# The last expert's rows kept apart: norm and store of all rows moved beside the last expert's matmuls

## The chip, the cores and the metric

The kernel runs on one core of one Trainium2 chip. The metric is device time in microseconds (us) of one whole execution; the kernel before took 3894.26 us (median of 3 runs, 3893.9 to 3895.97). All arithmetic here is in fp32.

## The reference

Two network blocks run one after the other on a sequence of 1024 tokens of 1024 features. The change touches only the end of the second block: a mixture of 16 experts in which each expert picks its own 128 tokens, and the final norm over all 1024 rows.

```python
def expert_choice_ffn(h, router_w, w_gate, w_up, w_down):
    cap = EC_CAPACITY * T // N_EXPERTS            # 2 * 1024 / 16 = 128
    aff = softmax(h @ router_w)
    gate, idx = lax.top_k(swapaxes(aff, 1, 2), cap)
    xe = h[idx]                                    # per expert: 128 rows
    hid = silu(xe @ w_gate) * (xe @ w_up)          # 1024 -> 512
    ye = (hid @ w_down) * gate                     # 512 -> 1024
    return zeros((T, D)).at[idx].add(ye)

# end of second_block
x = x + m_lat[5] * expert_choice_ffn(h_lat, ...)
return rms_norm(x, final_norm_g)                   # each row on its own
```

A token can be picked by several experts, so its row receives several additions. Within one expert's list every token stands once. The final norm needs the whole sum of a row.

## The kernel before, in words

The experts and the final norm are one function, `experts_and_norm`. Each of the five engines has an instruction list of its own, and they meet by semaphores; no scheduler moves anything, so the order of the code is the order on each engine.

**Experts.** For expert n, GpSimd (POOL) gathers 128 rows of `h` into `xe` with an indirect DMA. TensorE (PE) transposes them, and multiplies them with the gate weights (`ps_g`) and the up weights (`ps_u`), 8 matmuls of 128x512 each. ScalarE (ACT) takes the silu of `ps_g`, VectorE (DVE) multiplies it with `ps_u` into `hid`, PE transposes it into `ps_h`, ACT copies that to `hidT`, and PE multiplies with the down weights into the two banks `ps_d[0]` and `ps_d[1]`. DVE scales both banks into `ye`. POOL then adds `ye` onto the rows of `total` in DRAM with an accumulating indirect DMA (L5138; `total` is the tensor `x3`, which the profile prints as `x`). `added` counts these: the scatter of expert n waits until all n scatters before it have landed. PE goes on with the next expert meanwhile. Weights are double buffered; SyncE (SP) loads those of expert n + 2 when expert n is multiplied (L5051, L5052).

**Final norm.** SP waits until all 16 scatters have landed (`added` at 16 x 16), and then issues eight loads of 128 rows (512 KB each) into `tt` (L5109). For each of the eight tiles ACT squares with a sum (L5228) and takes the root (L5230); the first root needs another activation table than the silu. DVE takes the reciprocal (L5196) and multiplies the tile by it and by the gain (L5198). SP stores tile after tile to `out` as `normed` rises (L5112), waits for all stores, and the program ends.

Of the kernel before, what the change touches and what calls it, by code (L numbers as in the profile page):

```python
# [683 lines left out]
TILES = SEQ // P  # L684
# [4378 lines left out]
def experts_and_norm(nc, tag, h, idx, gates, weights, w_gate, w_up, w_down, total, ada, ada_bias, gate_at, gain, out):  # L5063
# [3 lines left out]
    with ExitStack() as ctx:  # L5067
# [14 lines left out]
        act_g, hid, hidT = sb("act_g", [P, FF]), sb("hid", [P, FF]), sb("hidT", [P, FB, P])  # L5082
        tt = sb("tt", [P, TILES, D])
        junk = sb("junk", [P, D], mybir.dt.bfloat16)
        ss, std, rstd, eps = (sb(n, [P, TILES]) for n in ("ss", "std", "rstd", "eps"))
        ps_t = [pbank("ps_t0"), pbank("ps_t1")]
        ps_g, ps_u, ps_h = pbank("ps_g"), pbank("ps_u"), pbank("ps_h")
# [5 lines left out]
        gathered = [sem("gathered0"), sem("gathered1")]  # L5093
        t_loaded = [sem(f"t_loaded{t}") for t in range(TILES)]
        stored = sem("stored")
        block = ctx.enter_context(nc.Block())

        @block.sync
        def _(sp):
            for n, src in enumerate((ada[0, gate_at:gate_at + D], ada_bias[gate_at:gate_at + D], gain)):  # L5100
                sp.dma_start(vecs[:, n, :], row_to_all(src, D)).then_inc(vecs_loaded, 16)
            with sp.Fori(0, EXPERTS // 2 - 1) as i:
                for b in range(2):

                    sp.wait_ge(d_made, 2 * i + b + 1)
                    load_expert(sp, weights, w_gate, w_up, w_down, 2 * i + (b + 2), b)
            sp.wait_ge(added, 16 * EXPERTS)
            for t in range(TILES):
                sp.dma_start(tt[:, t, :], total[t * P:(t + 1) * P, :]).then_inc(t_loaded[t], 16)  # L5109
            for t in range(TILES):  # L5110
                sp.wait_ge(normed, t + 1)
                sp.dma_start(out[t * P:(t + 1) * P, :], tt[:, t, :]).then_inc(stored, 16)  # L5112
            sp.wait_ge(stored, 16 * TILES)

        @block.gpsimd
        def _(pool):
            pool.memset(hold[:, :], 0.0)
            pool.memset(zero[:, :], 0.0)
            pool.memset(eps[:, :], EPS2)
            pool.drain()  # L5120

            def gather(b, e):


                pool.drain()
                pool.wait_ge(idx_set, e + 1)
                pool.tensor_tensor(hold[:, 0:1], zero[0:1, 0:1], zero[0:1, 0:1], ALU.add)
                pool.indirect_dma_start(out=xe[b][:, :], out_offset=None, in_=h,
                                        in_offset=bass.IndirectOffsetOnAxis(ap=idx_in[b][:, 0:1], axis=0)).then_inc(gathered[b], 16)

            def scatter(n, b):
                pool.drain()
                pool.wait_ge(y_done, n + 1)
                pool.tensor_tensor(hold[:, 0:1], zero[0:1, 0:1], zero[0:1, 0:1], ALU.add)

                pool.wait_ge(added, 16 * n)
                pool.tensor_tensor(hold[:, 1:2], zero[0:1, 0:1], zero[0:1, 0:1], ALU.add)
                pool.indirect_dma_start(out=total, out_offset=bass.IndirectOffsetOnAxis(ap=idx_out[b][:, 0:1], axis=0),  # L5138
                                        in_=ye[b][:, :], in_offset=None, compute_op=ALU.add).then_inc(added, 16)

            make_identity(pool, ident)
            pool.memset(ident[0:1, 0:1], 1.0).then_inc(consts, 1)
            gather(0, 0)
            gather(1, 1)
            with pool.Fori(0, EXPERTS // 2 - 1) as i:
                for b in range(2):
                    gather(b, 2 * i + (b + 2))
                    scatter(2 * i + b, b)
            scatter(EXPERTS - 2, 0)
            scatter(EXPERTS - 1, 1)  # L5150
            pool.wait_ge(added, 16 * EXPERTS)

        @block.vector
        def _(dve):
            def choose(b, e):

                dve.tensor_copy(idx_in[b][:, :], idx[:, bass.ds(e, 1)]).then_inc(idx_set, 1)

            choose(0, 0)
            choose(1, 1)  # L5160
            dve.wait_ge(vecs_loaded, 48)
            dve.tensor_tensor(vecs[:, 0, :], vecs[:, 0, :], vecs[:, 1, :], ALU.add)
            dve.drain()
# [26 lines left out]
                one(i, 0, True)  # L5190
                one(i, 1, True)
            one(EXPERTS // 2 - 1, 0, False)
            one(EXPERTS // 2 - 1, 1, False)
            for t in range(TILES):
                dve.wait_ge(std_done, t + 1)
                dve.reciprocal(rstd[:, t:t + 1], std[:, t:t + 1])  # L5196
                dve.drain()
                dve.scalar_tensor_tensor(out=tt[:, t, :], in0=tt[:, t, :], scalar=rstd[:, t:t + 1], in1=vecs[:, 2, :],  # L5198
                                         op0=ALU.mult, op1=ALU.mult).then_inc(normed, 1)

        @block.scalar
        def _(act):
            def move_x(n, b):
                for g in range(2):
                    act.wait_ge(turned, 2 * n + g + 1)
                    act.activation(xT[:, b, 4 * g:4 * g + 4, :], ps_t[g][:, :].rearrange("p (j c) -> p j c", j=4), ACT.Copy).then_inc(t_moved, 1)  # L5206

            def one(i, b, more):
                n = 2 * i + b
                act.wait_ge(g_made, n + 1)  # L5210
                act.wait_ge(hid_done, n)
                act.activation(act_g[:, :], ps_g[:, :], ACT.Silu).then_inc(g_act, 1)
                if more:
                    move_x(n + 1, 1 - b)
                act.wait_ge(h_turned, n + 1)
                act.wait_ge(d_made, n)
                act.activation(hidT[:, :, :], ps_h[:, :].rearrange("p (j c) -> p j c", j=FB), ACT.Copy).then_inc(h_moved, 1)  # L5217

            move_x(0, 0)
            with act.Fori(0, EXPERTS // 2 - 1) as i:  # L5220
                one(i, 0, True)
                one(i, 1, True)
            one(EXPERTS // 2 - 1, 0, True)
            one(EXPERTS // 2 - 1, 1, False)
            act.wait_ge(consts, 1)
            for t in range(TILES):
                act.wait_ge(t_loaded[t], 16)
                act.activation(junk[:, :], tt[:, t, :], ACT.Square, accum_out=ss[:, t:t + 1])  # L5228
                act.drain()
                act.activation(std[:, t:t + 1], ss[:, t:t + 1], ACT.Sqrt, scale=1.0 / D, bias=eps[:, 0:1]).then_inc(std_done, 1)  # L5230

        @block.tensor
        def _(pe):
# [9 lines left out]
                        last = pe.transpose(ps_t[g][:, j * P:(j + 1) * P], xe[b][:, k * P:(k + 1) * P], ident[:, :])  # L5243
                    last.then_inc(turned, 1)

            def one(i, b, more):
                n = 2 * i + b
                pe.wait_ge(gu_loaded[b], 32 * i + 32)
                pe.wait_ge(t_moved, 2 * n + 2)
# [18 lines left out]
                for g in range(2):  # L5268
                    for j in range(FB):
                        last = pe.matmul(ps_d[g][:, :], hidT[:, j, :], wd[:, b, j, g * BANK:(g + 1) * BANK], start=(j == 0), stop=(j == FB - 1))  # L5270
                last.then_inc(d_made, 1)

            turn(0, 0, 0)
            with pe.Fori(0, EXPERTS // 2 - 1) as i:
                one(i, 0, True)
                one(i, 1, True)
            one(EXPERTS // 2 - 1, 0, True)
            one(EXPERTS // 2 - 1, 1, False)


Z_WIDTH = 384
# [153 lines left out]
```

## Time and profile before

| What | us |
|---|---|
| Median of 3 runs | 3894.26 (3893.9 to 3895.97) |
| The profiled execution, its own time | 3900.91 |
| Its span (first to last instruction) | 3899.2 |
| PE busy in the span | 3479.7 (89%) |
| DVE, ACT, POOL busy | 1947.2 (50%), 1086.2 (28%), 1238.5 (32%) |

The profile is of one execution, 6.65 us above the median of the runs shown. Times in it count from the first instruction. A busy engine is one whose instructions run; waiting is not counted. The engine PE is busy nearly everywhere except in the last stretch, where it has nothing to do: its last matmul begins in a group at 3857.32 us and ends at 3864.5 us, 34.7 us before the span's end.

### The profile page before, as it was taken

The page shows a single profiled execution, that of the slowest core. Times are in us where ns is not written, and L with a number is a line of the kernel's source. Part 1 is how long each engine was busy: PE and PEld are TensorE (multiplying, and loading weights), DVE is VectorE, ACT ScalarE, POOL GpSimd, SP SyncE. Part 2 cuts the span into 40 slices and gives each one's busy share as a digit, 9 for nine tenths or more (in the row PEclk, how much of TensorE's full clock was granted, in tenths as well). Part 3 has the DMA queues.
Part 4 walks back from the last instruction along what each step waited for, and adds up shares of the span by engine and source line. Part 5 has one row for each costly group of instructions (what it writes and reads, how often), then busy time and mean ns, then how long its engine had stood idle before and what let it go on. Part 6 is the DMA issues. An engine that isn't in the chain of part 4 may idle for free. (4 is left out here: it accounts for less than half of the span.)

```text
span 3899.2 us, 47844 instructions
## 1 busy us (share of the span) xinstructions
PE 3479.7 (89%) x16721; PEld 2282.8 (59%) x16721; DVE 1947.2 (50%) x4099; ACT 1086.2 (28%) x2196; POOL 1238.5 (32%) x979
## 2 busy tenths in 40 slices
PE   8999998999798999999989798999977877939996
PEld 3745776777344676576657346575577874524442
DVE  2036663543783376667686453426588586141111
ACT  1024333441341233333342351322113112201111
POOL 2110101433343455556555452002302553201110
PEclk9999998999899999999999898999988878969998
DMA  4264543231532121221211643123325703438996
GB/s 134 79 181 132 168 122 100 87 108 64 220 146 65 59 59 42 63 58 53 74 41 37 250 161 92 44 79 106 126 76 180 252 33 143 163 127 288 315 317 227
DMA packets 417492, 494.07 MB, mean 127 GB/s; under 512 B 71042, under 2 KB 321178, under 8 KB 417267
## 3 DMA queue, kind: packets, MB, share of 16 engines
q1 hardware_dynamic: 390695, 463.64, 35.9%
q0 software_dynamic: 4608, 16.78, 1.7%
q10 hardware_dynamic: 21964, 10.75, 1.0%
q8 instruction: 129, 2.11, 0.2%
q14 instruction: 96, 0.79, 0.1%
HBM read 362.32 MB, written 128.77 MB: 126 GB/s over the span
## 5 line engine op out<-in xcount | busy, mean ns | idle before, releaser
L1091 POOL TENSOR_TENSOR hgrn_queries<-hgrn_qd,hgrn_pair_decay 128x640 f32<-128x640 f32 x192 | 262.7, 1387 | 293.5 <-PE hgrn_ps_a L1206 252.2
L1141 PE MATMUL hgrn_ps_w<-xT,hgrn_ring 128*128 128x512 f32 x432 | 196.4, 601 | 1.8 <-PEq L34 1.8
L415 PE MATMUL gla_bg_ps<-gla_bg_w,xT 128*128 128x256 f32 x768 | 186.2, 387 | 0.0
L554 POOL TENSOR_TENSOR l_wsum<-l_ring 128x512 f32<-128x512 f32 x14 | 20.0, 1430 | 507.4 <-PE att_bg_ps L586 185.6
L1757 PE MATMUL end_ps_z<-end_w,end_yT 128*128 128x512 f32 x384 | 168.8, 599 | 1.4 <-ACT end_yT L1700 1.4
L2927 PE MATMUL end_ps_z<-end_w,end_yT 128*128 128x512 f32 x384 | 166.8, 594 | 1.5 <-ACT end_yT L2847 1.5
L415 PEld LDWEIGHTS gla_bg_ps<-gla_bg_w,xT 128*128 128x128 f32 x768 | 145.7, 194 | 26.0 <-issue 6.8
L1311 DVE TENSOR_TENSOR hgrn_k_end<-hgrn_kd,hgrn_end_decay 128x128 f32<-128x128 f32 x168 | 136.2, 850 | 9.2 <-issue 2.6
L1141 PEld LDWEIGHTS hgrn_ps_w<-xT,hgrn_ring 128*128 128x128 f32 x432 | 81.7, 194 | 94.5 <-issue 94.2
L2205 ACT ACTIVATE att_s_sb<-att_s_sb,att_shift 128x256 f32<-128x256 f32 (+1 forms) x192 | 88.9, 464 | 166.2 <-DVE att_shift L2162 166.1
L1141 PE MATMUL hgrn_ps_w<-hgrn_xs,hgrn_wsum 128*128 128x512 f32 x288 | 130.0, 599 | 4.8 <-ACT hgrn_sig L1425 4.8
L1146 PE MATMUL hgrn_ps_w<-hgrn_ring,xT 128*128 128x256 f32 x576 | 129.7, 381 | 0.0
L1757 PEld LDWEIGHTS end_ps_z<-end_w,end_yT 128*128 128x128 f32 x384 | 73.0, 192 | 92.2 <-issue 89.1
L3328 PE MATMUL in_ps<-hT_cols,in_w 128*128 128x512 f32 x288 | 126.2, 592 | 0.0
L2172 DVE SCALAR_TENSOR_TENSOR att_acc<-att_w_ada,sT,att_acc 128x256 f32<-128x256 f32 x224 | 118.7, 543 | 14.3 <-issue 0.9
L2927 PEld LDWEIGHTS end_ps_z<-end_w,end_yT 128*128 128x128 f32 x384 | 72.3, 190 | 90.9 <-issue 87.8
L5270 PE MATMUL exp_ps_d<-expw_wd,exp_hidT 128*128 128x512 f32 x256 | 114.1, 599 | 11.0 <-ACT exp_hidT L5217 11.0
L1146 PEld LDWEIGHTS hgrn_ps_w<-hgrn_ring,xT 128*128 128x128 f32 x576 | 108.7, 192 | 14.5 <-issue 0.5
L2380 POOL TENSOR_TENSOR gla_queries<-gla_qd,gla_pair_decay 128x640 f32<-128x640 f32 x64 | 90.9, 1440 | 80.9 <-PE gla_ps_o L2446 57.2
L5252 PE MATMUL exp_ps_g<-expw_wg,exp_xT 128*128 128x512 f32 x256 | 115.4, 605 | 0.7 <-ACT exp_xT L5206 0.7
L2097 PE MATMUL att_ps_s<-att_k,att_q 64*128 64x256 f32 (+1 forms) x384 | 90.4, 553 | 25.5 <-DVE att_shift L2162 25.4
L5256 PE MATMUL exp_ps_u<-expw_wu,exp_xT 128*128 128x512 f32 x256 | 112.5, 592 | 0.0
(692 smaller groups left out, 7825.7 us busy)
## 6 DMA issues: line engine op xcount, KB each, us to landing
expw_wg<-in_exp_w_gate_dram SPq DMA_DIRECT2D x16, 2048.0 KB, 9.7
expw_wu<-in_exp_w_up_dram SPq DMA_DIRECT2D x16, 2048.0 KB, 16.3
expw_wd<-in_exp_w_down_dram SPq DMA_DIRECT2D x16, 2048.0 KB, 21.8
att_w_ada<-in_ada_w_dram SPq DMA_DIRECT2D x24, 1024.0 KB, 6.4
hgrn_ring<-in_w_in_c_dram SPq DMA_DIRECT2D x18, 1024.0 KB, 5.4
l_ring<-in_w_in_ab_dram SPq DMA_DIRECT2D x14, 1024.0 KB, 5.6
end_gt<-gate_l SPq DMA_DIRECT2D x16, 768.0 KB, 8.1
hgrn_ring<-in_w_in_c_dram SPq DMA_DIRECT2D x24, 512.0 KB, 5.2
```

What stands on the lines that cost most here:

```text
L415: last = pe.matmul(bank[0:job.rows, q * job.width:(q + 1) * job.width], job.acts[:, k, t * P:t * P + job.rows], w[:, k, 0:job.width], star ...
L1091: pool.tensor_tensor(queries[:, d, s, :].rearrange("p (b a c) -> p b a c", b=POINTS, a=PC), q, f, ALU.mult).then_inc(queries_done, 1)
L1141: last = pe.matmul(bank[:, :], a[:, k, :], x(k), start=(fresh and k == 0), stop=(k == HK - 1), skip_group_check=True)
L1146: last = pe.matmul(bank[:, q * 2 * P:(q + 1) * 2 * P], x(k)[:, t * P:(t + 1) * P], a[:, k, :], start=(fresh and q == 0 and k == 0), stop=( ...
L1311: dve.tensor_tensor(k_end[:, d, p % 2, :].rearrange("p (a c) -> p a c", c=CH), kd[:, b, d, t * P:(t + 1) * P].rearrange("p (a c) -> p a c" ...
L1757: made = pe.matmul(ps_z[h][:, :], yT[:, k, :], w[:, k, h * BANK:(h + 1) * BANK], start=(k == 0), stop=(k == NB - 1))
L2172: last = dve.scalar_tensor_tensor(out=mine, in0=w, scalar=s, in1=mine, op0=ALU.mult, op1=ALU.add)
L2927: made = pe.matmul(ps_z[h][:, :], yT[:, k, :], w[:, k, halves[h]], start=(k == 0), stop=(k == NB - 1))
L3328: last = pe.matmul(ps[(3 * n + part) % 2][:, 0:span], w[u % 3][:, k, b * P:(b + 1) * P], acts, start=(k == 0), stop=(k == KB - 1))
L5252: last = pe.matmul(ps_g[:, :], xT[:, b, k, :], wg[:, b, k, :], start=(k == 0), stop=(k == KB - 1))
L5256: last = pe.matmul(ps_u[:, :], xT[:, b, k, :], wu[:, b, k, :], start=(k == 0), stop=(k == KB - 1))
L5270: last = pe.matmul(ps_d[g][:, :], hidT[:, j, :], wd[:, b, j, g * BANK:(g + 1) * BANK], start=(j == 0), stop=(j == FB - 1))
```

## The change

Only the last expert (number 15, called FINAL) and the norm are written anew; experts 0 to 14 stay as they were.

- SP waits for 15 scatters instead of 16, and then loads the eight tiles of `tt`, which lack expert 15's contribution.
- ACT takes the silu of expert 15, then square and root of tile 0, then the copy to `hidT` of expert 15, and then the other seven tiles.
- DVE normalises tiles 0 to 3 behind `hid` of expert 15, then handles the first half of expert 15's result, tiles 4 and 5, the second half, tiles 6 and 7.
- POOL no longer adds expert 15 into `total`. When 15 scatters have landed it gathers expert 15's 128 rows of `total` into a new tile `rows`. DVE adds expert 15's scaled result to them (`last_half`), ACT and DVE norm them apart, and POOL scatters them to `out`, when all eight stores of SP have landed. It then waits for that scatter.
- PE signals each of the two banks of expert 15 (`last_made`) instead of both together (`d_made`).

So 128 of the 1024 rows are stored twice: first without expert 15 by the tile stores, and then complete by the scatter.

```diff
@@ sync
-            sp.wait_ge(added, 16 * EXPERTS)
+            sp.wait_ge(added, 16 * FINAL)
             for t in range(TILES):
                 sp.dma_start(tt[:, t, :], total[t * P:(t + 1) * P, :]).then_inc(t_loaded[t], 16)
@@ gpsimd
             scatter(EXPERTS - 2, 0)
-            scatter(EXPERTS - 1, 1)
-            pool.wait_ge(added, 16 * EXPERTS)
+            pool.drain()
+            pool.wait_ge(last_set, 1)
+            pool.tensor_tensor(hold[:, 0:1], zero[0:1, 0:1], zero[0:1, 0:1], ALU.add)
+            pool.wait_ge(added, 16 * FINAL)
+            pool.tensor_tensor(hold[:, 1:2], zero[0:1, 0:1], zero[0:1, 0:1], ALU.add)
+            pool.indirect_dma_start(out=rows[:, :], out_offset=None, in_=total,
+                                    in_offset=bass.IndirectOffsetOnAxis(ap=idx_last[:, 0:1], axis=0)).then_inc(rows_gathered, 16)
+            pool.drain()
+            pool.wait_ge(last_normed, 1)
+            pool.tensor_tensor(hold[:, 0:1], zero[0:1, 0:1], zero[0:1, 0:1], ALU.add)
+            pool.wait_ge(stored, 16 * TILES)
+            pool.tensor_tensor(hold[:, 1:2], zero[0:1, 0:1], zero[0:1, 0:1], ALU.add)
+            pool.indirect_dma_start(out=out, out_offset=bass.IndirectOffsetOnAxis(ap=idx_last[:, 0:1], axis=0),
+                                    in_=rows[:, :], in_offset=None).then_inc(last_stored, 16)
+            pool.wait_ge(last_stored, 16)
@@ vector
-            one(EXPERTS // 2 - 1, 1, False)
-            for t in range(TILES):
+            def normalise(t):
                 dve.wait_ge(std_done, t + 1)
                 dve.reciprocal(rstd[:, t:t + 1], std[:, t:t + 1])
                 dve.drain()
                 dve.scalar_tensor_tensor(out=tt[:, t, :], in0=tt[:, t, :], scalar=rstd[:, t:t + 1], in1=vecs[:, 2, :],
                                          op0=ALU.mult, op1=ALU.mult).then_inc(normed, 1)
+            def last_half(g):
+                c = slice(g * BANK, (g + 1) * BANK)
+                dve.wait_ge(last_made, g + 1)
+                dve.scalar_tensor_tensor(out=ye[1][:, c], in0=ps_d[g][:, :], scalar=gate_now[:, 1:2], in1=vecs[:, 0, c], op0=ALU.mult, op1=ALU.mult)
+                if g == 0:
+                    dve.wait_ge(rows_gathered, 16)
+                dve.drain()
+                dve.tensor_tensor(rows[:, c], rows[:, c], ye[1][:, c], ALU.add).then_inc(last_added, 1)
+
+            dve.tensor_copy(gate_now[:, 1:2], gates[:, FINAL:EXPERTS])
+            ...
+            dve.tensor_tensor(hid[:, :], act_g[:, :], ps_u[:, :], ALU.mult).then_inc(hid_done, 1)
+            dve.wait_ge(added, 16 * (FINAL - 1))
+            for t in range(TILES):
+                if t == 4:
+                    last_half(0)
+                if t == 6:
+                    last_half(1)
+                normalise(t)
+            dve.wait_ge(last_squared, 2)
+            dve.tensor_tensor(last_ss[:, 0:1], last_ss[:, 0:1], last_ss[:, 1:2], ALU.add).then_inc(last_summed, 1)
+            dve.wait_ge(last_root, 1)
+            dve.reciprocal(last_rstd[:, 0:1], last_std[:, 0:1])
+            dve.drain()
+            dve.scalar_tensor_tensor(out=rows[:, :], in0=rows[:, :], scalar=last_rstd[:, 0:1], in1=vecs[:, 2, :],
+                                     op0=ALU.mult, op1=ALU.mult).then_inc(last_normed, 1)
@@ scalar
-            one(EXPERTS // 2 - 1, 1, False)
-            act.wait_ge(consts, 1)
-            for t in range(TILES):
+            def root(t):
                 ...
+            act.activation(act_g[:, :], ps_g[:, :], ACT.Silu).then_inc(g_act, 1)
+            root(0)
+            act.wait_ge(h_turned, EXPERTS)
+            act.wait_ge(d_made, FINAL)
+            act.activation(hidT[:, :, :], ps_h[:, :].rearrange("p (j c) -> p j c", j=FB), ACT.Copy).then_inc(h_moved, 1)
+            for t in range(1, TILES):
+                root(t)
+            for g in range(2):
+                act.wait_ge(last_added, g + 1)
+                act.activation(junk[:, 0:BANK], rows[:, g * BANK:(g + 1) * BANK], ACT.Square, accum_out=last_ss[:, g:g + 1]).then_inc(last_squared, 1)
+                act.drain()
+            act.wait_ge(last_summed, 1)
+            act.activation(last_std[:, 0:1], last_ss[:, 0:1], ACT.Sqrt, scale=1.0 / D, bias=eps[:, 0:1]).then_inc(last_root, 1)
@@ tensor, in one(i, b, more, final=False)
-                last.then_inc(d_made, 1)
+                    if final:
+                        last.then_inc(last_made, 1)
+                if not final:
+                    last.then_inc(d_made, 1)
```

Where instructions stand on an engine is shown at three places, first before and then now. On ScalarE, from the silu of expert 15 on (`act_g` is the silu's result, `hidT` the transposed hidden tile, `ss` the sum of squares, `std` the root):

```order
L5212 ACTIVATE exp_act_g<-exp_ps_g 128x512
L5217 ACTIVATE exp_hidT<-exp_ps_h 128x512
L5228 ACTIVATE exp_junk,exp_ss<-exp_tt 128x1024
L5230 ACT_TABLE_LOAD
L5230 ACTIVATE exp_std<-exp_ss,exp_eps 128x1
```

```order
L5282 ACTIVATE exp_act_g<-exp_ps_g 128x512
L5275 ACTIVATE exp_junk,exp_ss<-exp_tt 128x1024
L5277 ACT_TABLE_LOAD
L5277 ACTIVATE exp_std<-exp_ss,exp_eps 128x1
L5286 ACTIVATE exp_hidT<-exp_ps_h 128x512
```

The square, the table load and the root of tile 0 now stand between the silu and the copy that PE's last eight matmuls wait for, and no second table load stands behind them.

On VectorE, from `hid` of expert 15 on (before, the rows shown run from `hid` to the first tile of the norm; now, from the fourth tile over the first half of expert 15 to the fifth tile):

```order
L5176 TENSOR_TENSOR exp_hid<-exp_act_g,exp_ps_u 128x512
L5180 COPY exp_idx_out<-idx 128x1
L5183 SCALAR_TENSOR_TENSOR exp_ye<-exp_ps_d,exp_gate_now,exp_vecs 128x512 x2
L5196 RECIPROCAL exp_rstd<-exp_std 128x1
L5198 SCALAR_TENSOR_TENSOR exp_tt<-exp_tt,exp_rstd,exp_vecs 128x1024
```

```order
L5217 SCALAR_TENSOR_TENSOR exp_tt<-exp_tt,exp_rstd,exp_vecs 128x1024
L5223 SCALAR_TENSOR_TENSOR exp_ye<-exp_ps_d,exp_gate_now,exp_vecs 128x512
L5227 TENSOR_TENSOR exp_rows<-exp_rows,exp_ye 128x512
L5215 RECIPROCAL exp_rstd<-exp_std 128x1
L5217 SCALAR_TENSOR_TENSOR exp_tt<-exp_tt,exp_rstd,exp_vecs 128x1024
```

The two scalings of `ps_d` are now two separate steps, each with an add, that stand ahead of tiles 4 and 6 of the norm.

On GpSimd, the end of its list, behind the scatter of expert 14:

```order
L5134 TENSOR_TENSOR exp_hold<-exp_zero 1x1
L5137 TENSOR_TENSOR exp_hold<-exp_zero 1x1
L5138 DMA x<-exp_ye,exp_idx_out 1024x1024
```

```order
L5157 TENSOR_TENSOR exp_hold<-exp_zero 1x1
L5159 TENSOR_TENSOR exp_hold<-exp_zero 1x1
L5160 DMA exp_rows<-x,exp_idx_last 128x1024
L5164 TENSOR_TENSOR exp_hold<-exp_zero 1x1
L5166 TENSOR_TENSOR exp_hold<-exp_zero 1x1
L5167 DMA out_dram<-exp_rows,exp_idx_last 1024x1024
```

One accumulating scatter has become a gather and, at the very end, a plain scatter to the output.

## Rows read from the trace of the kernel before

**Rows 1.** The chain that ended last, at its end: start us, us, what.
```profile
3848.31 0.60 ACT exp_act_g L5212
3857.32 7.15 PE exp_ps_d L5270 x16
3864.64 1.33 DVE exp_ye L5183 x2
3865.97 0.07 issue
3866.04 0.18 POOL exp_hold L5134
3866.53 6.06 DMA x<-exp_ye,exp_idx_out
3872.60 3.18 DMA exp_tt<-x
3877.07 1.28 ACT L5230
3889.04 1.28 DVE exp_tt L5198
```

**Rows 2.** DMA, 3873 to 3897 us: share of 16 engines in 40 slices, GB/s, queues, issues.
```profile
DMA  0999999999999997999999999999999999999411
GB/s 20 266 355 410 382 335 341 355 389 389 403 410 410 423 410 253 259 212 287 335 389 416 423 403 403 423 430 416 416 430 403 423 430 417 430 410 423 164 48 48
DMA packets 2303, 8.39 MB, mean 350 GB/s; under 512 B 255, under 2 KB 255, under 8 KB 2302
...
out_dram<-exp_tt SPq DMA_DIRECT2D x8, 512.0 KB, 7.3
```

**Rows 3.** The line of the stores, and DMA 3890.3 to 3891: last store's us to landing.
```profile
L5112 SPq DMA_DIRECT2D out_dram<-exp_tt x8: 332/333/338, 3880.2 to 3890.4; - x8
...
out_dram<-exp_tt SPq DMA_DIRECT2D x1, 512.0 KB, 7.2
```

**Rows 4.** Timeline of VectorE, hid of expert 15, and the norm's beat.
```profile
3855.24 0.69 DVE L5176 TENSOR_TENSOR exp_hid<-exp_act_g,exp_ps_u 128x512 f32<-128x512 f32 x1 [12.26 <-issue]
3864.56 1.40 DVE L5183 SCALAR_TENSOR_TENSOR exp_ye<-exp_ps_d,exp_gate_now,exp_vecs 128x512 f32<-128x512 f32 x2
...
3880.14 0.15 DVE L5196 RECIPROCAL exp_rstd<-exp_std 128x1 f32<-128x1 f32 x1
3880.36 1.28 DVE L5198 SCALAR_TENSOR_TENSOR exp_tt<-exp_tt,exp_rstd,exp_vecs 128x1024 f32<-128x1024 f32 x1
3881.57 0.15 DVE L5196 RECIPROCAL exp_rstd<-exp_std 128x1 f32<-128x1 f32 x1
```

**Rows 5.** Timeline of GpSimd: the scatter of expert 14, then that of 15.
```profile
3843.49 1.57 POOL L5138 DMA_INDIRECT x<-exp_ye,exp_idx_out  x1 [0.16 <-issue]
...
3866.19 0.18 POOL L5137 TENSOR_TENSOR exp_hold<-exp_zero 1x1 f32<-1x1 f32 x1
3866.53 1.56 POOL L5138 DMA_INDIRECT x<-exp_ye,exp_idx_out  x1 [0.16 <-issue]
```

**Rows 6.** DMA, 3840 to 3860 us, same columns as rows 2.
```profile
DMA  0000000000095899940000000000000000100000
...
x<-exp_ye,exp_idx_out POOLq DMA_INDIRECT x1, 6.3
```

**Rows 7.** The line of the tile loads, L5109: min/median/max us to landing.
```profile
L5109 SPq DMA_DIRECT2D exp_tt<-x x8: 344/462/1084, 3872.6 to 3877.1; - x8
...
DMA to landing us min/median/max: 3.2/7.3/10.1
```

**Rows 8.** Timeline of ScalarE: the copy of expert 15, then the norm's first two tiles.
```profile
3856.67 0.60 ACT L5217 ACTIVATE exp_hidT<-exp_ps_h 128x512 f32<-128x512 f32 x1 [7.76 <-PE exp_ps_h L5263]
3875.86 1.06 ACT L5228 ACTIVATE exp_junk<-exp_tt 128x1024 bf16<-128x1024 f32 x1 [18.59 <-DMA exp_tt<-x]
3876.82 0.19 ACT L5228 ACTIVATION_READ_ACCUMULATOR exp_junk<-exp_tt 128x1 f32 x1
3877.07 1.28 ACT L5230 ACT_TABLE_LOAD   x1
3878.36 0.29 ACT L5230 ACTIVATE exp_std<-exp_ss,exp_eps 128x1 f32<-128x1 f32 x1
3878.57 1.04 ACT L5228 ACTIVATE exp_junk<-exp_tt 128x1024 bf16<-128x1024 f32 x1
```

**Rows 9.** Indirect gathers, L5128, 3480 to 3500 us: us to landing, min/median/max.
```profile
L5128 POOL DMA_INDIRECT exp_xe<-h,exp_idx_in x3: 956/962/1223, 3482.9 to 3495.9; - x3
...
DMA to landing us min/median/max: 4.3/4.3/7.0
```

**Rows 10.** All 16 gathers (L5128) and all 16 scatters (L5138).
```profile
DMA to landing us min/median/max: 4.3/7.3/8.7
...
DMA to landing us min/median/max: 6.1/10.1/10.3
```

**Rows 11.** Stores of 512 KB of another stage, L4821.
```profile
L4821 SPq DMA_DIRECT2D h<-mix_out x8: 325/326/339, 3314.7 to 3429.0; - x8
...
DMA to landing us min/median/max: 2.6/2.6/7.0
```

**Rows 12.** Windows: stretch, busy us by engine, then PEclk, DMA share, GB/s.
```profile
3818.50:3838.50 20.00, 19.31 (x54) 9.06 (x53) 2.21 (x5) 2.25 (x4) 1.92 (x3) 1.00 0.94 324
3509.70:3864.50 354.80, 342.94 (x918) 158.67 (x916) 34.61 (x90) 42.07 (x67) 43.96 (x71) 1.00 0.84 290
3434.00:3509.60 75.60, 21.71 (x56) 11.05 (x57) 39.93 (x101) 3.38 (x5) 4.44 (x12) 0.57 0.13 44
```

More of the change, by code:

```diff
@@ L5084, in experts_and_norm @@
         junk = sb("junk", [P, D], mybir.dt.bfloat16)
+        rows, idx_last = sb("rows", [P, D]), sb("idx_last", [P, 1], I32)
+        last_ss, last_std, last_rstd = (sb(n, [P, 2]) for n in ("last_ss", "last_std", "last_rstd"))
         ss, std, rstd, eps = (sb(n, [P, TILES]) for n in ("ss", "std", "rstd", "eps"))
@@ L5095, in experts_and_norm @@
         stored = sem("stored")
+        last_set, rows_gathered, last_made, last_added, last_squared, last_summed, last_root, last_normed, last_stored = (sem(n) for n in (
+            "last_set", "rows_gathered", "last_made", "last_added", "last_squared", "last_summed", "last_root", "last_normed", "last_stored"))
+        FINAL = EXPERTS - 1
         block = ctx.enter_context(nc.Block())
@@ L5160, in _ @@
             choose(1, 1)
+            dve.tensor_copy(idx_last[:, :], idx[:, FINAL:EXPERTS]).then_inc(last_set, 1)
             dve.wait_ge(vecs_loaded, 48)
@@ L5199, in _ @@
                                          op0=ALU.mult, op1=ALU.mult).then_inc(normed, 1)
+            def last_half(g):
[7 more added lines that the diff above has]
+            dve.tensor_copy(gate_now[:, 1:2], gates[:, FINAL:EXPERTS])
+            dve.wait_ge(g_act, EXPERTS)
+            dve.wait_ge(u_made, EXPERTS)
+            dve.wait_ge(h_turned, FINAL)
+            dve.tensor_tensor(hid[:, :], act_g[:, :], ps_u[:, :], ALU.mult).then_inc(hid_done, 1)
[13 more added lines that the diff above has]
+                                     op0=ALU.mult, op1=ALU.mult).then_inc(last_normed, 1)
         @block.scalar
@@ L5230, in _ @@
                 act.activation(std[:, t:t + 1], ss[:, t:t + 1], ACT.Sqrt, scale=1.0 / D, bias=eps[:, 0:1]).then_inc(std_done, 1)
+            act.wait_ge(consts, 1)
+            act.wait_ge(g_made, EXPERTS)
+            act.wait_ge(hid_done, FINAL)
+            act.activation(act_g[:, :], ps_g[:, :], ACT.Silu).then_inc(g_act, 1)
[11 more added lines that the diff above has]
+            act.activation(last_std[:, 0:1], last_ss[:, 0:1], ACT.Sqrt, scale=1.0 / D, bias=eps[:, 0:1]).then_inc(last_root, 1)
         @block.tensor
@@ L5244, in turn, with one @@
                     last.then_inc(turned, 1)
-            def one(i, b, more):
+            def one(i, b, more, final=False):
                 n = 2 * i + b
@@ L5277, in _ @@
             one(EXPERTS // 2 - 1, 0, True)
-            one(EXPERTS // 2 - 1, 1, False)
+            one(EXPERTS // 2 - 1, 1, False, True)
 Z_WIDTH = 384
```

## The prediction

> **What bounds the kernel now.** I read the page's busy shares first (TensorE 89%, so most of the program is TensorE's), then the chain of waits at the place of the change. That chain shows the end of the kernel as a serial tail in which TensorE does nothing: from the last matmul at 3864.5 us to the span's end at 3899.2 us lie 34.7 us [rows 1]. Its pieces are: DVE's scaling 1.5, POOL and the accumulating scatter 6.6 (3865.97 to 3872.60), the first tile's load 3.2, squares and first root with its table load 2.9, eight tiles of DVE at one per 1.43 us until 3890.33, and the last store. I then read the DMA view of 3873 to 3897 us: 8.39 MB move with the 16 DMA engines full in nearly every slice [rows 2]. So tail stores queue behind each other and behind loads; the last, issued at 3890.4, lands 7.2 us later, at 3897.6 [rows 3], and the program ends 1.6 us after it. Last, the DMA view of 3840 to 3860 us: the queues are empty beside the scatter of expert 14, while TensorE multiplies expert 15 [rows 6]. That is where the change puts the loads.
>
> **Experts 0 to 14.** Nothing changes there but one 128x1 copy on DVE at the start (0.15 us, beside waiting). The loop ends as before, and I keep its times.
>
> **Start of the loads.** The scatter of expert 14 starts at 3843.49 [rows 5] and takes 6.3 us [rows 6]: it lands at 3849.8. SP's queue holds nothing else then, so the eight loads start at 3849.8 instead of 3872.60. That is 22.8 us earlier, which is the most that the change could give if all else followed at once.
>
> **ACT, tile 0 and `hidT`.** The first load took 3.2 us [rows 7], so tile 0 is there at 3853.0; the silu ended at 3848.9 [rows 1]. Square, sum, table load and root took from 3875.86 to 3878.65, 2.8 us [rows 8]: until 3855.8. `hidT` waits for its transposes and started at 3856.67 [rows 8]. So root(0) lies in ACT's idle time with 0.85 us to spare, and TensorE isn't held. The cover is thin: every microsecond by which tile 0 lands later than 3.2 + 0.85 delays `hidT`, TensorE's last group of matmuls and all other roots by as much. Nothing is queued behind the wait on ACT but these.
> What the trace shows of the table load is 1.28 us and 0.06 us of issue ahead of it [rows 1, 8].
> The Trainium skill (ScalarE: Activation LUTs, What ACT_TABLE_LOAD costs) adds a drain of about 1.38 us to each switch. By the page, estimated, root(0) would end at 3857.2, `hidT` would be 0.6 us late and the gain 0.6 us smaller; the trace has no such gap at this very switch, so my sum leaves it out.
>
> **ACT, tiles 1 to 7.** They follow `hidT` (3857.27) at 1.40 us each (the second square starts at 3878.57 [rows 8], and DVE, fed by the roots, keeps 1.43 [rows 4]), with root(1) done 1.5 us after its start: 3858.8, then to 3867.2 for tile 7. The loads keep ahead: at the 350 GB/s of [rows 2] 4.2 MB take 12 us, and 13.5 with the 0.5 MB gather; tile 7 is needed at 3865.7.
>
> **DVE.** `hid` ends at 3855.93 [rows 4]. Tile 0 goes 3855.9 to 3857.5, then DVE waits for root(1) at 3858.8. From there a tile costs 1.43 us (3880.14 to 3881.57) [rows 4]. Each half of expert 15 costs a scaling, 0.74 (1.40 for two that overlap), a drain of about 0.07 and an add of 0.69 (taken from `hid`, the same shape): 1.5 us. The halves start at 3863.1 and 3867.5. `ps_d[0]` is ready at 3857.32 + 3.6 = 3860.9 and `ps_d[1]` at 3864.5, so neither waits. The gather of `rows` starts with about 0.5 us for POOL at 3850.3; gathers took 4.3 us with free queues [rows 9] and at most 8.7 beside weight loads [rows 10]: it lands at 3859 at the latest, 4 us ahead of need. Tile 7 is normed at 3858.8 + 7 x 1.43 + 2 x 1.5 + 0.1 = 3871.9. Without the two halves it would be 3868.9.
>
> **The last store.** Issued at 3872.0 instead of 3890.4. Stores now come from DVE at 1.43 us and more apart, while 512 KB take 1.3 us at the 410 GB/s of the full slices [rows 2]. The loads and the gather are through by 3863.5, and the four stores then waiting by 3869, so tile 7 meets a nearly empty queue. Bounds: 2.6 us for a store with free queues [rows 11], 7.2 for one in a full queue [rows 3]. I take 3.0, near the first: landed at 3875.0.
>
> **The last 128 rows.** ACT's second half-square runs beside tiles 6 and 7. After tile 7, DVE's sum 0.2, ACT's root 0.35, reciprocal, drain and scaling 1.55: `rows` is ready at 3874.0, 1.0 us before the stores have landed. So the stores decide, not the norm. POOL then needs about 0.4 us (3866.19 to 3866.53 before) [rows 5], and scatters from 3875.4. The trace has no plain scatter. Below: a gather of the same 128 rows, 4.3 [rows 9]. Above: the accumulating scatter, 6.1 at the least, which reads before it writes, and 10.1 beside loads [rows 10]. There are no loads then. Its issue is 0.6 us longer than a gather's (1.57 against 0.96) [rows 5, 9], which makes 4.9 my value, nearest the gather. Landed at 3880.3, and 1.6 us to the end: 3881.9.
> [...]
>
> **Sum.** 3899.2 - 3881.9 = 17.3 us less span. The profiled execution took 3900.91, so it would take 3883.6; the runs shown have a median 6.65 us below that: 3894.26 - 17.3 = 3877.0 us. In terms: loads earlier 22.8, minus two halves 2.9, minus ACT's pause before tile 1 (root(1) ends 5.8 us after load 0 has landed, before 4.3) 1.5, minus POOL and scatter 5.3, plus a store that doesn't queue 4.2.
>
> **Rivals.**
> (a) *DMA and tile 0 go as in the full stretch.* Tile 0 lands later, ACT is held in root(0), `hidT` and the roots slip; and the last store queues. For it: thin cover of 0.85 us, the gather of `rows` and the tile loads start in the same microsecond, so 0.5 MB more shares the DMA engines. Against: the first load before had seven others behind it too. Price: tile 0 at 5.2 instead of 3.2 costs 1.2; a last store at 7.2 costs 4.2 more; a scatter of 6.1 costs 1.2. Together 6.6: 3883.6 us.
> (b) *The plain scatter is as dear as the loaded one*, 10.1: 5.2 more, 3882.2 us. With (a)'s store it is 3886.4, the edge of what is told from no change. It has no loads beside it, so this is unlikely.
> (c) *Slower: TensorE's clock.* The experts run at the full level, 2.4 GHz (granted 1.00 over 354.8 us), and the 75.6 us before them, in which TensorE was busy 21.7 us, at 0.57 [rows 12]. TensorE fills these 354.8 us; if the new build were granted 1.2 GHz in part of them, each microsecond so spent costs half of one. It decides from 35 us at the lower level on; a stretch of 75 us would cost 38 and give 3915 us. For it: the clock is granted by the chip, not set. Against: nothing before 3848 changes, and TensorE's own gaps stay.
> (d) *TensorE slows beside the tile loads.* It ran 19.31 of 20 us beside weight loads that took 0.94 of the DMA engines [rows 12], so I give it nothing.
> (e) *The old tail stays*, because something still waits for expert 15 before the stores. The order shows all eight tile norms independent of it except through DVE's two halves, so it costs 3 us, already counted.
>
> **How the numbers follow.** This kernel's measurement tells 0.2%, some 7.8 us, from no change. My forecast 0.76, with its own range of 3875.0 to 3880.5 (store 2.6 to 5, scatter 4.3 to 6.1, tile 0 up to 1 us late). (a) 0.13, (b) 0.05, (c) 0.03, anything else that leaves it within 0.2%: 0.03. The range reaches up to (a): 3874.8 to 3883.8. Faster by over 0.2%: forecast, (a) and most of (b), 0.93. Same 0.04, slower 0.03.
>
> **What would show it.** Tile loads issued at about 3849.8, square of tile 0 at 3853, `hidT` still at 3856.7 (at 3857.3 or later, the cover was too thin). TensorE's last matmul still ends at 3864.5. DVE in one beat from 3858.8 to 3872 with no wait but the one before tile 1. The last tile store lands 3 us after issue. POOL's wait is ended by the stores and not by DVE. The plain scatter takes 4.3 to 6.1 us, and the span ends 1.6 us later, near 3882. The prediction is wrong if DVE waits for `rows` or for `ps_d`, if ACT holds TensorE, or if the stretch before 3843 us moves.

## The result, and the profile after

The changed kernel took 3873.22 us (median of 4 runs, 3870.82 to 3873.76) against 3895.11 us before (4 runs, 3893.9 to 3897.46): ratio 0.9947, 95% interval 0.9935 to 0.9958. Faster, as forecast, but by 21.9 us where 17.3 were forecast. The forecast was 3877.0 us; the result lies 1.8 us below its own range (3875.0 to 3880.5) and 1.6 us below the range with rival (a) in it (3874.8 to 3883.8).

The end of the chain of waits of the changed kernel, in the columns of [rows 1] (`...` stands for pieces left out):

```profile
3838.95 0.61 ACT exp_act_g L5282
...
3849.53 1.28 DVE exp_tt L5217
...
3861.38 1.30 DVE exp_tt L5217
3862.68 0.02 issue
3862.70 3.65 DMA out_dram<-exp_tt
3866.34 0.07 issue
3866.41 0.18 POOL exp_hold L5166
3866.59 0.16 issue
3866.75 1.00 POOL out_dram L5167
```

The accumulating scatter (6.06) and the first tile's load (3.18) are gone from the chain. VectorE's tiles now stand beside the last expert, and the tail store (7.2 in [rows 3]) has become 3.65. The timeline of GpSimd has the three issues that matter, and that of SyncE the loads and stores:

```profile
3834.08 1.59 POOL L5143 DMA_INDIRECT x<-exp_ye,exp_idx_out  x1 [0.16 <-issue]
...
3841.44 1.00 POOL L5160 DMA_INDIRECT exp_rows<-x,exp_idx_last  x1 [0.39 <-issue]
...
3866.41 0.18 POOL L5166 TENSOR_TENSOR exp_hold<-exp_zero 1x1 f32<-1x1 f32 x1 [1.52 <-DMA out_dram<-exp_tt]
3866.75 1.00 POOL L5167 DMA_INDIRECT out_dram<-exp_rows,exp_idx_last  x1 [0.16 <-issue]
```

```profile
3840.57 4.00 SPq L5114 DMA_DIRECT2D exp_tt<-x  x8
3848.44 14.59 SPq L5117 DMA_DIRECT2D out_dram<-exp_tt  x8
```

Here is the surprise. The scatter of expert 14 belongs to code that the change doesn't touch, and it is issued at 3834.08, where [rows 5] has 3843.49. So the two profiled spans differ by 27.2 us: 9.4 ahead of the change and 17.8 in it. (The medians differ by less, 21.9 us, because the profiled execution of the kernel before was a long one.) Measured from that scatter's issue to the end of the span, the tail was 55.7 us and is 37.9.

| From the issue of the scatter of expert 14 | before | forecast | after |
|---|---|---|---|
| tile loads issued | 29.1 | 6.3 | 6.5 |
| `hidT` of expert 15 | 13.2 | 13.2 | 13.2 |
| second tile begun on DVE | 36.7 | 15.3 | 15.2 |
| tile 7 normed, store issued | 46.9 | 28.5 | 28.6 |
| last tile store landed | 54.1 | 31.5 | 32.3 |
| plain scatter issued | - | 31.9 | 32.7 |
| plain scatter landed | - | 36.8 | 36.1 |
| end of the span | 55.7 | 38.4 | 37.9 |

ScalarE around the copy, to set beside [rows 8]:

```profile
3843.99 1.06 ACT L5275 ACTIVATE exp_junk<-exp_tt 128x1024 bf16<-128x1024 f32 x1 [4.44 <-DMA exp_tt<-x]
3844.95 0.19 ACT L5275 ACTIVATION_READ_ACCUMULATOR exp_junk<-exp_tt 128x1 f32 x1
3845.19 1.28 ACT L5277 ACT_TABLE_LOAD   x1
3846.49 0.29 ACT L5277 ACTIVATE exp_std<-exp_ss,exp_eps 128x1 f32<-128x1 f32 x1
3847.26 0.60 ACT L5286 ACTIVATE exp_hidT<-exp_ps_h 128x512 f32<-128x512 f32 x1 [0.48 <-PE exp_ps_h L5327]
```

ScalarE waited 0.48 us for `ps_h` after the root of tile 0. The cover (the idle time of ScalarE in which the root of tile 0 hides) held, with half of the 0.85 us that I had given it. And the DMA view from 3841 to 3865 us, to set beside [rows 2]:

```profile
DMA  1599999999999999999999999999999999899897
...
DMA packets 2442, 8.91 MB, mean 371 GB/s; under 512 B 270, under 2 KB 270, under 8 KB 2440
```

The DMA engines are as full as they were, now from the first load to the last store: the last two slices still have 9 and 7 tenths, where I had forecast a nearly empty queue for the last store.

### The profile page after: what moved, and what is told of

Its sections match the earlier page's. It is cut to its first block and busy times, and to the rows that moved or that the text cites. A ratio compares the mean times of both kernels' runs of the same rounds, so it can differ in the third digit from the quotient of the medians.

```text
span 3872.0 us, 47862 instructions
## 1 busy us (share of the span) xinstructions
PE 3474.3 (90%) x16721; PEld 2277.8 (59%) x16721; DVE 1949.0 (50%) x4104; ACT 1088.4 (28%) x2201; POOL 1242.9 (32%) x982
## 6 DMA issues: line engine op xcount, KB each, us to landing
expw_wd<-in_exp_w_down_dram SPq DMA_DIRECT2D x16, 2048.0 KB, 21.9
```

## The experiments

Theory A: the change is worth its tail, about 18 us, and what lies ahead of it takes a different time in every execution. Theory B: the changed program is also faster ahead of expert 15, by the same amount each time. "Tail" is always the time from the issue of the scatter of expert 14 to the end of the span, read from the run's one profile. Ratios are to the kernel before, run in the same session.

**e1: the kernel before, unchanged.**

> The kernel before, unchanged. Theory A (drift): the stages ahead of expert 15 take a different time from execution to execution, because the granted clock falls and rises at other places in the stretch from 2680 to 3060 us; the change is worth only its tail, 17.8 us. Then the scatter of expert 14 is issued anywhere between 3834 and 3844 us in this profile, and the ratio to the kernel before is 1.000 within 0.0015. Theory B (build): the changed program is faster ahead of expert 15 by a fixed amount. Then the scatter of expert 14 is issued at 3843.5 +- 1.5 us here, as in the first trace of before. Both expect 55.7 +- 0.5 us from that issue to the end of the span.

Ratio 0.9998 (0.9987 to 1.0008), 12 runs from 3886.24 to 3899.76. Scatter of expert 14 at 3839.50, tail 55.4. The same program was 4.0 us earlier at that scatter than in the first trace: theory A's kind of difference, larger than B allows.

**e2: the changed kernel, unchanged.**

> The changed kernel, unchanged. Theory A (drift): ratio to before between 0.9944 and 0.9960 (17.8 us is 0.9954), issue of the scatter of expert 14 anywhere between 3834 and 3844 us. Theory B (build): ratio 0.9944 or below again, and that issue at 3834 +- 1.5 us. Both expect 37.9 +- 0.5 us from that issue to the end of the span.

Ratio 0.9953 (0.9940 to 0.9965), 5 runs from 3871.31 to 3875.32. Scatter at 3832.53, tail 37.1. The two signs point to different theories: the ratio is A's, though its interval reaches B's 0.9944, and the scatter is 1.5 us earlier than A allowed and just inside B's 3834 +- 1.5. The tail came out 0.3 us shorter than the 37.4 to 38.4 expected of both, because the last store landed 2.9 us after its issue and not 3.65.

**e3: only the declarations of the change.**

```diff
+        rows, idx_last = sb("rows", [P, D]), sb("idx_last", [P, 1], I32)
+        last_ss, last_std, last_rstd = (sb(n, [P, 2]) for n in ("last_ss", "last_std", "last_rstd"))
+        last_set, rows_gathered, last_made, last_added, last_squared, last_summed, last_root, last_normed, last_stored = (sem(n) for n in (
...
+            dve.tensor_copy(idx_last[:, :], idx[:, FINAL:EXPERTS]).then_inc(last_set, 1)
```

> The kernel before with only the new tiles, the nine new semaphores and the one 128x1 copy of the last expert's indices. Theory A (drift): ratio 1.000 within 0.0015. Theory B (build), in the form that the new declarations or the moved addresses do it: ratio 0.9985 to 0.9990 (4 to 6 us faster), and the scatter of expert 14 issued near 3834 us. The tail of 55.7 us stays under both.

Ratio 1.0003 (0.9992 to 1.0015), scatter at 3837.46, tail 55.5. New tiles, semaphores and moved addresses give nothing beyond 0.1%, so theory B in this form is out.

**e4: the loads held back.**

```diff
             sp.wait_ge(added, 16 * FINAL)
+            sp.wait_ge(last_made, 2)
@@ scalar
-            root(0)
...
-            for t in range(1, TILES):
+            for t in range(TILES):
                 root(t)
```

> The changed kernel with the tile loads held back until both banks of expert 15 are multiplied, and root(0) behind the copy to hidT (it would wait for itself otherwise). If the gain comes from moving the tile loads beside expert 15's matmuls: loads issue 14.5 us later, tile 0 is normed about 13 us later, the stores again share the DMA engines with the loads and the last one lands 3 to 4 us later after its issue: 37.9 + 16.5 = 54 to 55 us from the issue of the scatter of expert 14 to the end, ratio to before 0.9990 to 1.0005. Rival: the gain comes from not waiting for the last scatter (6.6 us) and not from the overlap: then some 44 us and a ratio near 0.997.

Ratio 0.9988 (0.9978 to 0.9998), tail 50.6. The first two rows are SyncE's, the third is VectorE's first tile:

```profile
3854.64 3.73 SPq L5115 DMA_DIRECT2D exp_tt<-x  x8
3862.35 13.61 SPq L5118 DMA_DIRECT2D out_dram<-exp_tt  x8
```

```profile
3861.03 1.28 DVE L5218 SCALAR_TENSOR_TENSOR exp_tt<-exp_tt,exp_rstd,exp_vecs 128x1024 f32<-128x1024 f32 x1
```

Loads at 21.1 us after the scatter instead of 6.5, and tile 7 13.4 us later, as expected. But the last store landed 3.2 us after its issue, not 7, and the tail is 3.4 us shorter than the 54 expected at the least. From the first load's issue to the last store's issue 21.0 us pass, where 17.8 passed before, and the two halves are 3.0 of that; so the stores come slowly enough for the queue to empty (no run of e4 without the halves shows it apart). Of the 18 us, then, 13.0 come from the overlap (50.6 against a mean of 37.6 in four profiles of the changed kernel; e4 moves root(0) too, which alone cost 2.05 in e6), and some 5 are left when nothing overlaps. Those 5 are a sum: the loads 8.1 us earlier, since no scatter of expert 15 stands ahead of them, and a last store that lands 4.0 us faster; against that 3.2 more up to the last store's issue, and 3.7 more behind its landing, where the plain scatter now stands. The overlap is most of the gain; of the rival's 11.5 us, less than half came.

**e5: the changed kernel again.**

> The changed kernel once more. Theory A (drift: the stages ahead take what the clock gives them in each execution, the same for both programs): median ratio to before 0.9954 +- 0.001, and with more runs the spread grows to that of before, 10 us and more between lowest and highest. Theory B (this program is steadier and some 3 us faster ahead of expert 15): ratio 0.9946 or below, all runs again within 5 us. Both expect 37.1 to 37.9 us from the issue of the scatter of expert 14 to the end of the span.

Ratio 0.9949 (0.9932 to 0.9965), 6 runs from 3869.04 to 3880.80, scatter at 3832.72, tail 37.9. The spread grew to 11.8 us, which takes away the narrow times of theory B. The ratio lies inside A's 0.9944 to 0.9964 and just above B's 0.9946; its interval holds both.

**e6: `root(0)` behind the copy to `hidT`** (the ScalarE part of e4's diff alone).

> The changed kernel with root(0) behind the copy to hidT instead of ahead of it. If the beat of VectorE, which starts at the second tile's root, sets the tail: square, table load and root of tile 0 (2.9 us) now come after hidT, every tile is normed 2.8 us later, and the tail is 40.3 us instead of 37.5. Rival: the DMA engines, full from the first load to the last store, set the tail, and VectorE's delay is hidden in them: tail 38.0 us or less.

Ratio 0.9966 (0.9954 to 0.9978), tail 39.65. VectorE's tiles 1 to 7 all came 2.8 us later, as the first theory said. The last store then took 2.6 us to land instead of the 2.9 to 3.65 of the changed kernel, so 2.05 us of it were lost in the end (39.65 against the mean of 37.6), between the 40.3 of the one theory and the 38.0 of the other. Both have their part: VectorE's beat (its steady 1.43 us for each tile), cushioned by full DMA engines. This is also the price of the cover: were root(0) not hidden ahead of `hidT`, 2 us of the gain would be gone.

**e7: both halves of expert 15 behind tile 7. e8: the first ahead of tile 7, the second behind.**

```diff
             for t in range(TILES):
-                if t == 4:
-                    last_half(0)
-                if t == 6:
-                    last_half(1)
                 normalise(t)
+            last_half(0)
+            last_half(1)
```

```diff
             for t in range(TILES):
-                if t == 4:
+                if t == 7:
                     last_half(0)
-                if t == 6:
-                    last_half(1)
                 normalise(t)
+            last_half(1)
```

> The changed kernel with both halves of expert 15 behind tile 7 on VectorE. If VectorE's beat alone set the last store, it would be issued 2.9 us earlier and land 2.9 us earlier; then the last rows decide, ready about 1 us ahead of the old landing: tail 0.7 us shorter. Rival: the DMA engines are full, the last store is issued 2.9 us earlier but lands at most 1 us earlier (landing 5.5 us or more after issue instead of 3.65): tail shorter by 0.7 us as well, but the wait ahead of the scatter is then ended by the store or within 0.3 us of it.

> The changed kernel with the first half of expert 15 ahead of tile 7 and the second behind it. The last store is issued 1.4 us earlier than in the changed kernel; the rows are ready at the same time as in e7. Both theories of e7 expect a tail 0.7 us shorter than the changed kernel's; if the DMA engines set the store's landing, it comes within 0.5 us of that in e7 although it is issued 1.5 us later.

e7: ratio 0.9950 (0.9934 to 0.9966), tail 38.0. e8: 0.9959 (0.9944 to 0.9974), tail 37.9. No gain in either, where both theories had expected a tail 0.7 us shorter. The last store's landing, from the views of the DMA issues around it, first e7, then e8:

```profile
out_dram<-exp_tt SPq DMA_DIRECT2D x1, 512.0 KB, 6.3
```

```profile
out_dram<-exp_tt SPq DMA_DIRECT2D x1, 512.0 KB, 5.1
```

In the changed kernel, e8 and e7 the last store is issued 28.6, 27.2 and 26.1 us after the scatter of expert 14, and it lands at 32.3, 32.3 and 32.4 us. When VectorE finishes doesn't matter in this span of 2.5 us. (With the issue always at 28.6, the landing itself lies between 31.5 and 32.3 in the four profiles of the changed kernel.) The rival of e7 held in what it said of the store, and so did e8's landing within 0.5 us of e7's; the shorter tail that went with them did not come.

**e9: as e7, the stores of tiles 0, 2 and 4 left out.** Part of the output is then not written. The two waits for all stores count five instead of eight (not shown).

```diff
             for t in range(TILES):
-                sp.wait_ge(normed, t + 1)
-                sp.dma_start(out[t * P:(t + 1) * P, :], tt[:, t, :]).then_inc(stored, 16)
+                if t not in (0, 2, 4):
+                    sp.wait_ge(normed, t + 1)
+                    sp.dma_start(out[t * P:(t + 1) * P, :], tt[:, t, :]).then_inc(stored, 16)
```

> As e7 (both halves of expert 15 behind tile 7), and the stores of tiles 0, 2 and 4 are left out, so part of the output isn't written; 1.5 MB less go through the DMA engines. If full DMA engines held the last store in e7 (6.3 us from issue to landing), it now lands 2.6 to 3.7 us after issue; the last rows then decide, and the tail from the issue of the scatter of expert 14 is 37.3 to 37.7 us. Rival: a store's landing near the end is slow for another reason than traffic; then it stays at 6 us.

Ratio 0.9951 (0.9932 to 0.9969), only 2 runs. The last store landed 2.6 us after its issue, 28.4 us after the scatter: 4.0 us earlier than in e7. The 1.5 MB left out are 3.9 us at some 400 GB/s, but that the two agree is partly luck: 2.6 us is what a store takes with free DMA engines [rows 11], so here its issue sets the landing and no longer the bytes. The wait ahead of the final scatter was then ended by the rows:

```profile
3868.88 0.18 POOL L5165 TENSOR_TENSOR exp_hold<-exp_zero 1x1 f32<-1x1 f32 x1 [23.47 <-DVE exp_rows L5245]
3869.02 0.18 POOL L5167 TENSOR_TENSOR exp_hold<-exp_zero 1x1 f32<-1x1 f32 x1
```

Tail 36.9, 0.4 under the 37.3 to 37.7 expected. So traffic holds the last store of the changed kernel: its landing is bound by the bytes from the first load on. The tail as a whole is held only a little by them. With the store 4.0 us earlier it became 1.1 us shorter than in e7, because the rows of expert 15 come right behind, and e6 shows that a later VectorE costs at once.

**e10: experts 14 and 15 both apart.** The way tried next is to start the bytes earlier. Rows of expert 14 (`pre_rows`) are treated like those of expert 15 and scattered ahead of them, and VectorE and ScalarE handle all eight tiles ahead of expert 15's silu and `hid`.

```diff
-            sp.wait_ge(added, 16 * FINAL)
+            sp.wait_ge(added, 16 * (FINAL - 1))
@@ gpsimd
+            for t in range(TILES):
+                pool.wait_ge(t_loaded[t], 16)
+            pool.tensor_tensor(hold[:, 0:1], zero[0:1, 0:1], zero[0:1, 0:1], ALU.add)
             scatter(EXPERTS - 2, 0)
...
+            pool.indirect_dma_start(out=pre_rows[:, :], out_offset=None, in_=total,
+                                    in_offset=bass.IndirectOffsetOnAxis(ap=idx_out[0][:, 0:1], axis=0)).then_inc(pre_gathered, 16)
...
+            pool.indirect_dma_start(out=out, out_offset=bass.IndirectOffsetOnAxis(ap=idx_out[0][:, 0:1], axis=0),
+                                    in_=pre_rows[:, :], in_offset=None).then_inc(pre_stored, 16)
```

> Experts 14 and 15 both kept apart: the tile loads start when 14 scatters have landed and end before the scatter of expert 14, all eight tiles are normed before hid of expert 15, and the rows of expert 14 and of expert 15 are gathered, normed and scattered one after the other. If the tail of the changed kernel is held by the 8.9 MB that move from the first load on, starting them one expert earlier takes it away: the last matmul's end to the end of the span falls from 16.9 us to some 12.6 us, and the ratio to before is near 0.9943. Rival: the longer chain on GpSimd (two gathers, two scatters, about 4 us each) takes the place of the stores, and that time stays at 16 us or more.

Ratio 0.9964 (0.9952 to 0.9976), 6 runs with a mean of 3878.8: 4.0 us above the changed kernel in the same session (e11), with an uncertainty of about 1.4. GpSimd's timeline says part of why:

```profile
3844.84 2.55 POOL L5146 DMA_INDIRECT x<-exp_ye,exp_idx_out  x1 [0.16 <-issue]
3854.30 0.18 POOL L5164 TENSOR_TENSOR exp_hold<-exp_zero 1x1 f32<-1x1 f32 x1 [6.92 <-issue]
...
3855.02 1.00 POOL L5167 DMA_INDIRECT exp_rows<-x,exp_idx_last  x1 [0.39 <-issue]
3856.33 0.98 POOL L5169 DMA_INDIRECT exp_pre_rows<-x,exp_idx_out  x1 [0.30 <-issue]
...
3866.27 1.00 POOL L5176 DMA_INDIRECT out_dram<-exp_pre_rows,exp_idx_out  x1 [0.16 <-issue]
3870.05 0.18 POOL L5180 TENSOR_TENSOR exp_hold<-exp_zero 1x1 f32<-1x1 f32 x1 [2.78 <-DVE exp_rows L5265]
...
3870.54 1.00 POOL L5183 DMA_INDIRECT out_dram<-exp_rows,exp_idx_last  x1 [0.16 <-issue]
```

The scatter of expert 14 had to wait for the tile loads, which shared the engines with expert 15's weights, until 3843. Its landing (3854.1) and the two gathers then stood in a row. But the final scatter did not wait for the one ahead of it, which had landed at 3869.6: its wait was ended at 3870.05 by VectorE. The chain shows what stood between the second gather and the end:

```profile
3856.33 5.01 DMA exp_pre_rows<-x,exp_idx_out
...
3861.36 1.06 ACT exp_junk L5308
...
3862.56 1.28 ACT L5310
...
3864.42 1.28 DVE exp_pre_rows L5257
...
3866.44 0.70 DVE exp_rows L5243
...
3868.68 1.29 DVE exp_rows L5265
```

The norm of expert 14's rows, with a table load (the 1.28 us of L5310) that the changed kernel doesn't have there, stood on ScalarE and VectorE ahead of expert 15's second half. `hid` came late too, behind the tiles, and TensorE waited 1.9 us for it where it had waited 0.8. From the last matmul's end (3857.9) to the end 17.9 us passed, against 16.9 in the first profile of the changed kernel (16.1 to 16.9 in its four). The rival of e10 held in its time, 16 us or more, and half in its reason: two gathers in a row, but not two scatters. None of the versions tried beats the changed kernel.

**e11: the changed kernel a fourth time.**

> The changed kernel a fourth time. Theory A (drift): the mean over its runs stays 17.8 +- 2.5 us below that of the kernel before on the same chip, and the issue of the scatter of expert 14 lies anywhere between 3828 and 3846 us. Theory B (3 us more ahead of expert 15): 20.5 us or more below again.

Ratio 0.9953 (0.9939 to 0.9966), mean 3874.8 over 5 runs against 3892.1 of before: 17.3 us. Scatter of expert 14 at 3837.66, tail 37.5. Both signs are theory A's.

**All runs together.** Taking each program's tail from its mean time leaves what lies ahead: before 3893.34 - 55.55 = 3837.8 (53 runs, spread 21.8 us; 3838.0 if the 28 runs of the first comparison, e1 and e3 are added); changed 3873.58 - 37.60 = 3836.0 (20 runs, spread 11.8 us); e4, e6, e7 and e8, which share all that lies ahead with it, 3838.0 (31 runs). With standard deviations of 4.9 and 2.9 us the 1.8 us between the first two has an uncertainty of about 0.9. The third group shows no such gain (its own uncertainty is 0.8), which speaks against theory B without ruling out a microsecond of it.

## Why the prediction was right or wrong

*Start of the loads, ACT and tile 0, `hidT`, DVE:* right, each within 0.4 us. The order of the table holds line by line. The Trainium skill (ScalarE: Activation LUTs, What ACT_TABLE_LOAD costs), which the prediction cited, has a drain of 1.38 us more at each switch of the activation table. The trace does not agree: 0.05 us lie between the sum's read and the load, and `hidT` wasn't late.

*The gather:* 7.8 us, inside its bounds, never waited for. *The loads:* 15.8 us from the first issue to the last landing, where I had counted 13.5.

*The last store:* 3.65, 2.9, 3.6 and 3.3 us in the profiles of the changed kernel, e2, e5 and e11, against 3.0. The size was nearly right and the reason wrong. I had the loads through by 3863.5 and the stores by 3869 in the first trace's time, with an empty queue after it; e7 and e8, which issue it earlier and gain nothing, and e9, where fewer bytes free it, show that the engines stay full to its landing. The 3.65 is not a free store's landing but the end of the bytes, which happened to fall there. I should have divided 8.9 MB by 400 GB/s (22.3 us; 24.0 at the mean of 371 GB/s that the trace then showed) and set it against the 22.1 us from first load to last issue: so near that neither alone is the bound.

*The plain scatter:* 3.4 us, below my lower bound of 4.3 and against the 4.9 in the sum. A gather of the same rows isn't a floor for it. Its issue is 1.00 us, like a gather's, and not 1.57: that belongs to the accumulating form. The end then takes 1.85 us instead of 1.6.

*Sum:* 17.3 forecast, 17.8 in the first pair of profiles. That they are so near is partly luck: the scatter was 1.5 us too dear, and the store (0.65), its issue (0.1) and the end (0.25) were too cheap. The tails are 55.7, 55.4 and 55.5 before (the last that of e3) and 37.9, 37.1, 37.9 and 37.5 after: means 17.95 us apart.

*Where it failed:* the part "Experts 0 to 14", where I kept the times of the old trace and gave them no width, and the range built from it. The prediction had named the sign, "if the stretch before 3843 us moves", and it moved: the scatter of expert 14 was issued 9.4 us earlier, and lies anywhere from 3826.2 (e8) to 3839.6 (e7) in nine profiles of programs that share all ahead of it. In the first comparison 4 us of the 21.9 came from there and not from the tail. The time of the kernel before differs by 21.8 us between its 53 runs; I had three of them within 2 us and took the profiled 3900.91 for the price of profiling. It was only another execution: every run lies 1.7 to 1.8 us above its own span, and among the profiled ones are the fastest of their group (e2, e6, e8) as well as the slowest (e7, e9, e11). The own range of 3875.0 to 3880.5 held the tail's unknowns alone. Against the mean of all 20 runs of the changed kernel, 3873.6, the forecast of 3877.0 is 3.4 us too high: 0.9 is the median of three runs taken for the 3893.3 of 53, 0.65 is the tail, and 1.8 is the remainder above, which no run explains.

*What the drift is.* Over the 53 runs of before, time and mean granted clock (0.939 to 0.945) correlate at -0.61. The traces show where some of the 9.4 us arise. A matmul group of an earlier stage and the one behind it, first in the trace of before, then in that of after:

```profile
2690.18 2.93 PE L3853 MATMUL gdnp_ps_r<-mask,logs 128*128 128x128 f32 x12 [3.83 <-DVE gdnp_dec L3929]
2692.91 3.52 PE L411 MATMUL gdnp_bg_ps<-hT,gdnp_bg_w 128*128 128x512 f32 x4
```

```profile
2688.30 1.60 PE L3853 MATMUL gdnp_ps_r<-mask,logs 128*128 128x128 f32 x12 [1.65 <-DVE gdnp_dec L3929]
2689.74 1.88 PE L411 MATMUL gdnp_bg_ps<-hT,gdnp_bg_w 128*128 128x512 f32 x4
```

Ahead of these rows the kernel before was 0.3 us the earlier one, behind them it is 4.8 us the later one. TensorE waited 2.2 us longer and then ran both groups at nearly twice the time, 3.0 us more: the granted clock was 0.66 from 2688 to 2698 us, and 1.00 from 2686 to 2694 us in the trace of after. It is the execution and not the program, for e4, which shares this code with the changed kernel, has the same wait of 3.83 and the same 2.93 us. The stage at L4215 adds 2.0 us, in the same order:

```profile
L4215 PE MATMUL gdnl_ps_a<-gdnl_R,gdn_H x120: 274/414/552, 2888.7 to 3007.6; 128*128 128x128 f32 x120
```

```profile
L4215 PE MATMUL gdnl_ps_a<-gdnl_R,gdn_H x120: 274/275/550, 2884.1 to 3001.0; 128*128 128x128 f32 x120
```

It lasts 118.9 us in the one and 116.9 in the other; the other 4.6 us of the difference at its end were there at its start. The median of its matmuls is 414 ns in one and 275 in the other, but that doesn't decide the stage's time: in e5 the median is 421 ns and the stage lasts 115.4 us, in e2 it is 275 and the stage lasts 118.6. So the clock is a part of the drift, and waits between the engines that fall differently in each execution are another. How the two divide the 9.4 us stays open, and so does whether 1 or 2 us of the changed kernel's gain truly lie ahead of the change.

*Rivals.* (a) had the right mechanism for the store, DMA engines full to the end, and a price far too high: 4.2 us, where 0.65 came. (b), (d) and (e) did not come. (c), the clock, is real in both directions, but outside the experts: their stretch kept the full clock in both traces (granted 1.00 from 3509.7 to 3864.5 us before and from 3500 to 3855 us after). I had priced it only as a rare loss of 35 us and more, not as a few microseconds in every run.

## What to carry to other kernels

A tail of loads, norm and stores can be started a whole expert earlier if the rows that the last expert still changes are kept apart; count the bytes from the first load to the last store against the engines' rate before reordering anything else inside it. A difference of a few microseconds in a 3.9 ms program is read in the trace from a common instruction ahead of the change to the end, not from two medians. Before giving a range, take the spread of more runs than three, and put it into the range beside the unknown costs.

## What the runs showed of the hardware

A plain indirect scatter of 128 rows of 4 KB landed 3.3 to 3.4 us after its issue began in all profiles that have one, with an issue of 1.00 us; the accumulating one took 6.0 at the least (e3), and 1.57 to issue [rows 5, 10]. In e10, GpSimd's 1x1 operation, 0.18 us elsewhere, took 1.17; the second row is what VectorE did at the time:

```profile
3843.37 1.17 POOL L5142 TENSOR_TENSOR exp_hold<-exp_zero 1x1 f32<-1x1 f32 x1 [0.15 <-issue]
```

```profile
3843.21 1.28 DVE L5233 SCALAR_TENSOR_TENSOR exp_tt<-exp_tt,exp_rstd,exp_vecs 128x1024 f32<-128x1024 f32 x1 [0.46 <-issue]
```

It ended at 3844.54, 0.05 us after VectorE's operation with two SBUF inputs (3844.49), and the scatter's issue next to it took 2.55 instead of 1.59. The Trainium skill (SBUF — State Buffer, SBUF: two separate sides) says that such a VectorE operation and a GpSimd operation that reads SBUF exclude each other for a whole instruction; this row agrees, and it is the only one of its kind here.
